# Memory attention of a decoder step: scores issued two units ahead of the turns, the low halves last, and the sample products moved to GpSimd

## The reference

```python
def memory_attention(h, mem_k, mem_v, w_mq, w_mo):
    q = jnp.einsum('btd,dhe->bthe', h, w_mq)
    s = jnp.einsum('bthe,bmhe->bhtm', q, mem_k).astype(jnp.float32) * (MEM_HDIM ** -0.5)
    p = jax.nn.softmax(s, axis=-1).astype(mem_v.dtype)
    o = jnp.einsum('bhtm,bmhe->bthe', p, mem_v)
    return jnp.einsum('bthe,hed->btd', o, w_mo)
```

## Time and profile before

| | |
|---|---|
| median of three runs | 1979.57 us |
| span of the profiled execution | 1973.4 us |
| what lies around the span (the difference) | 6.2 us |
| TensorE busy in the span | 95% |
| VectorE busy | 62% |
| ScalarE busy | 29% |
| GpSimd busy | 28% |
| mean granted TensorE clock | 0.985 of full speed |

### The profile page before, as it was taken

How to read it: one execution, slowest core, us unless ns; L and a number is a source line. 1 busy time by engine, 2 the same in 40 slices (tenths; PEclk the granted TensorE clock), 3 DMA queues, 4 the chain that set the end, 5 groups by cost and what they waited for, 6 DMA issues and landing times.

```text
span 1973.4 us, 35022 instructions
## 1 busy us (share of the span) xinstructions
PE 1875.2 (95%) x15121; PEld 1617.4 (82%) x15121; DVE 1215.5 (62%) x1579; ACT 567.5 (29%) x962; POOL 547.0 (28%) x384
## 2 busy tenths in 40 slices
PE   7999999998899899999998699998999999999999
PEld 7988888884566444448997589998999999999998
DVE  5585583675677888875433746884377177375475
ACT  5222221244444455552121332110011011021026
POOL 2212211240000243423224013433333333333540
PEclk8999999998999999999999899999999999999999
DMA  7211211133000798943124402111211211211202
GB/s 237 53 46 33 55 45 33 30 74 120 1 1 1 293 339 329 337 172 129 33 86 150 160 22 65 43 43 34 64 44 34 63 43 33 65 38 38 86 22 89
DMA packets 162310, 176.77 MB, mean 90 GB/s; under 512 B 21982, under 2 KB 146932, under 8 KB 157772
## 3 DMA queue, kind: packets, MB, share of 16 engines
q1 hardware_dynamic: 146240, 93.54, 16.1%
q0 software_dynamic: 7168, 75.50, 10.0%
q10 hardware_dynamic: 8750, 5.49, 0.9%
HBM read 161.33 MB, written 13.27 MB: 88 GB/s over the span
## 4 chain that ended last, share of the span: by engine, by line
PE 79%; DVE 13%; ACT 4%; issue 2%; DMA 1%; POOL 1%; ACTq 0%; DVEq 0%; POOLq 0%; SPq 0%
PE PS L769 18%; PE PS L771 18%; PE PS L770 18%; PE PS L1060 4%; PE PS L806 4%; PE PS L1093 3%; PE PS L1001 2%; PE PS L850 2%; DVE ct L2366 2%; PE PS L979 2%; PE PS L1050 1%; PE PS L1075 1%; DVE Sst L1939 1%; DVE small L2126 1%; DVE ct L2386 1%
## 5 line engine op out<-in xcount | busy, mean ns | idle before, releaser
L715 POOL CAST whi<-wraw 128x1024 fp32r<-128x1024 f32 (+4 forms) x142 | 139.9, 985 | 1019.4 <-PE PS L771 905.7
L769 PE MATMUL PS<-BH,whi 128*128 128x344 f32 x1152 | 368.9, 320 | 0.0
L770 PE MATMUL PS<-BL,whi 128*128 128x344 f32 x1152 | 367.1, 319 | 0.0
L771 PE MATMUL PS<-BH,wlo 128*128 128x344 f32 x1152 | 367.0, 319 | 0.0
L717 POOL TENSOR_TENSOR wlo<-wraw,whi 128x1024 fp32r<-128x1024 f32 (+4 forms) x142 | 309.1, 2177 | 11.4
L770 PEld LDWEIGHTS PS<-BL,whi 128*128 128x128 f32 x1152 | 216.2, 188 | 0.5 <-issue 0.5
L769 PEld LDWEIGHTS PS<-BH,whi 128*128 128x128 f32 x1152 | 216.2, 188 | 0.5 <-issue 0.5
L771 PEld LDWEIGHTS PS<-BH,wlo 128*128 128x128 f32 x1152 | 216.2, 188 | 0.0
L769 PE MATMUL PS<-XH,whi 128*128 128x344 f32 x528 | 180.3, 341 | 3.4 <-DVE XL L1826 3.4
L2274 DVE TENSOR_TENSOR XT<-PS,XT 128x1032 f32<-128x1032 f32 x48 | 59.2, 1232 | 179.7 <-PE PS L771 179.6
L770 PE MATMUL PS<-XL,whi 128*128 128x344 f32 x528 | 169.6, 321 | 0.0
(11 more groups left out here) (445 smaller groups left out, 3729.3 us busy)
## 6 DMA issues: line engine op xcount, KB each, us to landing
wraw<-in_w_up_dram SPq DMA_DIRECT2D x44, 512.0 KB, 3.9
wraw<-in_w_in_dram SPq DMA_DIRECT2D x20, 512.0 KB, 4.1
wraw<-in_w_down_dram SPq DMA_DIRECT2D x24, 256.0 KB, 2.8
wraw<-in_w_down_dram SPq DMA_DIRECT2D x16, 320.0 KB, 3.1
xt_kept<-XT SPq DMA_DIRECT2D x1, 4128.0 KB, 13.4
XT<-xt_kept SPq DMA_DIRECT2D x1, 4128.0 KB, 13.5
xstage<-in_x_prompt_dram SPq DMA_DIRECT2D x8, 512.0 KB, 10.1
wraw<-in_w_out_dram SPq DMA_DIRECT2D x8, 512.0 KB, 4.7
```

Source lines behind the costliest of these rows:

```text
L715: gp.tensor_copy(hi, raw).then_inc(w_hi_done, 1)
L769: pe.matmul(out, wh[:, t, 0:m], hi[:, tile(t), s], start=(t == first), stop=False)
L770: pe.matmul(out, wh[:, t, 0:m], low, start=False, stop=False)
L771: ins = pe.matmul(out, wl[:, t, 0:m], hi[:, tile(t), s], start=False, stop=(t == last))
```

## The change

Four things move together.

TensorE's unit becomes scores(n + 2), turn(n), values(n - 1): the scores no longer stand behind the turn and its wait. `keep_busy` is gone, 75 transposes in all. The banks of the scores get a counter of their own (`freed["ms"]`), as the order of scores and turns now differs between TensorE and ScalarE.

VectorE's unit becomes max(n + 2), scale(n + 1), the sample work, low(n - 1).

The product of keys and query goes to GpSimd, in place in the key buffer; VectorE keeps the sum. There are three key buffers, and the sample rows are taken in units 4 to 11 without a gap.

The softmax of the sample scores on VectorE and the turn on TensorE stand one unit later (12, 13, 14, 15 where 11, 12, 13, 14 stood on VectorE). On TensorE only the turn of the sample scores moves, from unit 11 to 12.

```diff
-            use(("ms", n), [n % 2], "s")
+            use(("ms", n), [n % 2], "ms")
...
-            use(("mpt", n), [2 + n % 2], "s")
             if n + 2 < len(munits):
                 plan_ms(n + 2)
+            use(("mpt", n), [2 + n % 2], "s")
...
-        sample_at = {2: 0, 3: 1, 4: 2, 6: 3, 7: 4, 8: 5, 9: 6, 10: 7}
+        sample_at = {4 + b: b for b in range(NS)}
...
-                        if b >= 2:
-                            sp.wait_ge(prod_done, b - 1)
-                            sp.dma_start(sK[b % 2][:, :, :], i["cache_mem_k"][0, b].rearrange("(t p) h e -> p t (h e)", p=P)).then_inc(sk_in[b % 2], 16)
+                        if b >= 3:
+                            sp.wait_ge(prod_done, b - 2)
+                            sp.dma_start(sK[b % 3][:, :, :], i["cache_mem_k"][0, b].rearrange("(t p) h e -> p t (h e)", p=P)).then_inc(sk_in[b % 3], 16)
...
+            def sample_products(b):
+                gp.wait_ge(sk_in[b % 3], 16 * (b // 3 + 1))
+                gp.tensor_tensor(sK[b % 3][:, :, :], sK[b % 3][:, :, :], QB[b][:, :].unsqueeze(1).broadcast_to([P, 2, ME]), ALU.mult).then_inc(prod_new, 1)
...
+                if j == job_no[("mo", 0)]:
+                    gp.wait_ge(q_in, 16 * NS)
+                    for b in range(NS):
+                        sample_products(b)
                 split_weight(j)
...
-                if n < 14:
-                    keep_busy(7, 6 if n < 11 else 3)
+                if n + 2 < len(munits):
+                    memory_scores(n + 2)
                 pe.wait_ge(m_new, n + 1)
                 turn(("mpt", n), [Pm[n % 2][:, hh, m * P:m * P + P] for hh in range(2) for m in range(2)])
-                if n + 2 < len(munits):
-                    memory_scores(n + 2)
                 if n:
                     memory_values(n - 1)
-                if n == 11:
+                if n == 12:
                     pe.wait_ge(prod_done, NS)
...
+                if n + 2 < len(munits):
+                    memory_max(n + 2)
                 if n + 1 < len(munits):
                     memory_scale(n + 1)
-                if n + 2 < len(munits):
-                    memory_max(n + 2)
-                if n:
-                    memory_low(n - 1)
                 if n in sample_at:
                     b = sample_at[n]
-                    ve.wait_ge(q_in, 16 * NS)
-                    ve.wait_ge(sk_in[b % 2], 16 * (b // 2 + 1))
-                    step(ve.tensor_tensor(prod[:, :, :], sK[b % 2][:, :, :], bc(QB[b][:, :], 1, 2), ALU.mult))
-                    ve.tensor_reduce(sc[:, :, MH * b:MH * b + MH], prod[:, :, :].rearrange("p t (h e) -> p t h e", h=MH), AX, ALU.add).then_inc(prod_done, 1)
-                    ve.wait_ge(prod_done, b + 1)
+                    ve.wait_ge(prod_new, b + 1)
+                    ve.tensor_reduce(sc[:, :, MH * b:MH * b + MH], sK[b % 3][:, :, :].rearrange("p t (h e) -> p t h e", h=MH), AX, ALU.add).then_inc(prod_done, 1)
...
+                if n:
+                    memory_low(n - 1)
```

More of the change, by code:

```diff
@@ L193, in build_program @@
         Pm = [Pm0, Pm1]
-        mko, PTm0, PTm1, QS, prod, sc, scr, pm, sK0, sK1, *sV = place(
+        mko, PTm0, PTm1, QS, prod, sc, scr, pm, sK0, sK1, sK2, *sV = place(
             B0, B1, ("mko", [P, 2, ME], F32), ("PTm0", [P, 4, P], F32), ("PTm1", [P, 4, P], F32), ("QS", [NS, ME], F32),
@@ L197, in build_program @@
             ("pm", [P, 2, 32], F32), ("sK0", [P, 2, ME], F32), ("sK1", [P, 2, ME], F32),
-            *[(f"sV{n}", [P, 2, ME], F32) for n in range(NS)])
-        PTm, sK = [PTm0, PTm1], [sK0, sK1]
+            ("sK2", [P, 2, ME], F32), *[(f"sV{n}", [P, 2, ME], F32) for n in range(NS)])
+        PTm, sK = [PTm0, PTm1], [sK0, sK1, sK2]
         QB = place(S0, A0, *[(f"QB{n}", [P, ME], F32) for n in range(NS)])
@@ L217, in build_program @@
         psum_full = {"d": sem("dense_full"), "r": sem("rec_full")}
-        freed = {n: sem(f"freed_{n}") for n in ("v", "s", "rv", "rs")}
+        freed = {n: sem(f"freed_{n}") for n in ("v", "s", "ms", "rv", "rs")}
         ident_in, consts_in = sem("ident_in"), sem("consts_in")
@@ L245, in build_program @@
         m_max, m_new, om_hi = sem("m_max"), sem("m_new"), sem("om_hi")
-        sk_in, sv_in = [sem(f"sk_in{n}") for n in range(2)], sem("sv_in")
+        sk_in, sv_in, prod_new = [sem(f"sk_in{n}") for n in range(3)], sem("sv_in"), sem("prod_new")
         q_out, q_in, qs_set, prod_done, s_max, s_exp, s_new2 = sem("q_out"), sem("q_in"), sem("qs_set"), sem("prod_done"), sem("s_max"), sem("s_exp"), sem("s_new2")
@@ L256, in build_program @@
         p_max, p_new = sem("p_max"), sem("p_new")
-        uses, nth, last_of = {}, {"d": 0, "r": 0, "v": 0, "s": 0, "rv": 0, "rs": 0}, {}
+        uses, nth, last_of = {}, {"d": 0, "r": 0, "v": 0, "s": 0, "ms": 0, "rv": 0, "rs": 0}, {}
         def use(key, banks, by):
@@ L653, in _ @@
                     full(sp, ("mq", MH - 1))
-                    for b in range(2):
+                    for b in range(3):
                         sp.dma_start(sK[b][:, :, :], i["cache_mem_k"][0, b].rearrange("(t p) h e -> p t (h e)", p=P)).then_inc(sk_in[b], 16)
@@ L1191, in memory_scores @@
                 end(ins)
-            def keep_busy(b, count):
-                for r in range(count):
-                    pe.transpose(PS[:, b, P * (r % 3):P * (r % 3) + P], ident[:, :], ident[:, :])
             def memory_values(n):
@@ L1666, in memory_exp @@
                                          bias=small[:, c:c + 1], accum_out=small[:, 8 + c:9 + c])
-                ins.then_inc(freed["s"], 1)
+                ins.then_inc(freed["ms"], 1)
             memory_exp(0)
@@ L2328, in _ @@
             for n in range(len(munits)):
+                if n + 2 < len(munits):
+                    memory_max(n + 2)
                 if n + 1 < len(munits):
                     memory_scale(n + 1)
-                if n + 2 < len(munits):
-                    memory_max(n + 2)
-                if n:
-                    memory_low(n - 1)
                 if n in sample_at:
                     b = sample_at[n]
-                    ve.wait_ge(q_in, 16 * NS)
-                    ve.wait_ge(sk_in[b % 2], 16 * (b // 2 + 1))
-                    step(ve.tensor_tensor(prod[:, :, :], sK[b % 2][:, :, :], bc(QB[b][:, :], 1, 2), ALU.mult))
-                    ve.tensor_reduce(sc[:, :, MH * b:MH * b + MH], prod[:, :, :].rearrange("p t (h e) -> p t h e", h=MH), AX, ALU.add).then_inc(prod_done, 1)
-                    ve.wait_ge(prod_done, b + 1)
-                elif n == 11:
+                    ve.wait_ge(prod_new, b + 1)
+                    ve.tensor_reduce(sc[:, :, MH * b:MH * b + MH], sK[b % 3][:, :, :].rearrange("p t (h e) -> p t h e", h=MH), AX, ALU.add).then_inc(prod_done, 1)
+                elif n == 12:
                     full(ve, "sct")
                     ve.tensor_reduce(small[0:32, 40:41], bank("sct")[0:32, 0:MT], AX, ALU.max, negate=True).then_inc(s_max, 1)
-                elif n == 12:
+                elif n == 13:
                     emptied(ve, "sct")
@@ L2348, in _ @@
                     ve.tensor_scalar(scr[0:32, :], scr[0:32, :], small[0:32, 42:43], None, ALU.mult).then_inc(s_new2, 1)
-                elif n == 13:
+                elif n == 14:
                     full(ve, "spt")
                     take(ve.tensor_copy(pm[:, :, :].rearrange("p m n -> p (m n)"), bank("spt")[:, 0:64]))
-                elif n == 14:
+                elif n == 15:
                     full(ve, "spv")
                     take(ve.tensor_copy(prod[:, :, :], PS[:, uses["spv"][1][0]:uses["spv"][1][0] + 2, :]))
+                if n:
+                    memory_low(n - 1)
             memory_low(len(munits) - 1)
```

## The result

| | median us | runs | ratio to before | 95% interval |
|---|---|---|---|---|
| before, beside it | 1978.78 | 4 | | |
| changed | 1952.86 (1950.26 to 1958.99) | 4 | 0.9877 | 0.9856 to 0.9898 |
| changed, measured again | 1954.34 (1948.52 to 1957.91) | 5 | 0.9868 | 0.9849 to 0.9888 |

The last row was measured beside a median of 1980.75 for the kernel before. The change made the kernel some 24 to 26 us faster, 1.2 to 1.3%. The forecast was a gain of 16.3.

A forecast was written before the change was run, and what follows sets the result against it. It took the loop as bound by a chain of waits across engines, no engine being full. 4.9 + 21.1 - 9.2 - 0.5 = 16.3 us gain, 1979.6 - 16.3 = 1963.3 us; 8-in-10 range 1953 to 1972.

The forecast's parts named there:

- the likeliest case: Whole kernel: gain of 12 to 20 us, time 1959.5 to 1967.5, chance 0.62.
- in step: GpSimd's products fall while VectorE does other work, no scale held: gain 26.0 - 0.5, time 1954.1, chance 0.17.
- the loop of about 51 us: Sign of being right: the loop over the 16 units, 67.44 us before, would take about 51 us.
- the long scales of 1.5 to 3 in about every second unit: Sign of being right: VectorE's scales in units 3 to 11, otherwise 0.69 us, lengthened about every second time.
- Plain unit 3.19 to 2.37: VectorE's new order hides scale and reciprocal in its wait for ScalarE: 0.82 us in each of 6 units, 4.9 us.
- Sample unit 5.69 to 3.05: Sample product off VectorE, round over ScalarE hidden: 2.64 us saved in each of 8 units, 21.1 us.
- Holds, 8 x 2.3 / 2 = 9.2: VectorE's scale waits for a GpSimd product in every second sample unit, 2.3 us each: costs 9.2 us.
- Clock, 0.5: TensorE in the loop, without the fill of transposes, sometimes drops to half clock: costs 0.5 us.
- The rival of a clock that stays down: Without the fill TensorE stays at 1.2 GHz from early in the loop: 7.6 us slower, 1987.2, chance 0.05.
- Reloads hidden with 2.6 to spare: Key reload some 4.2 us plus product 2.4 makes 6.6, its row wanted three units later at 9.2: no cost.
- Tail 8.46, weights' splits in time: Loop's end to first dense output product stays 8.46 us; GpSimd's output-weight splits hidden by 11 us and more.
- Around the span, 6.2: Profiled execution lies 6.2 us under the median of the runs, and the same distance was expected after the change.

The follow-up runs named there:

- tiny products: Changed kernel with each GpSimd product cut to one element in 1024 per partition: stage 48.41 us, median 1952.55 us.
- late first product: Changed kernel with one 128x1024 memset on GpSimd between the queries' arrival and the first product: stage 51.06 us, median 1955.66 us.
- two buffers: Changed kernel with two key buffers in place of three: stage 58.81 us, median 1960.11 us.
- doubled product: Changed kernel with each GpSimd product made twice, first into a scratch tile: stage 67.06 us, median 1970.76 us.
- the run with the scale on ScalarE: Changed kernel with the scales of units 5 to 12 made by ScalarE, reciprocals left on VectorE: stage 47.66 us, median 1950.34 us.
- the last run on the other chip: Changed kernel with scales of units 5 to 12 on ScalarE and the last five value loads behind the last key reload: 1978.49 us, ratio 0.9853.

## Why the prediction was off in size

The direction, the place and all the mechanisms of gain were right; the likeliest case was not. The forecast of 1963.3 priced 16.3 us, the runs show 24 to 26, and the rival "in step" with 1954.1 is what happened. The medians of the changed kernel, 1952.86 and 1954.34, lie at the low end of the range given, 1953. Of the signs named, the loop of about 51 us (41.93) and the long scales of 1.5 to 3 in about every second unit (one of 16) failed.

- *Plain unit 3.19 to 2.37:* 2.38 measured. Right.
- *Sample unit 5.69 to 3.05:* 2.85 measured. The instructions that follow one another on VectorE overlap by 0.08 at four places and not at two; the remaining 0.03 is a hundredth of a microsecond in each of three terms. Eight times 0.2: 1.6 us more than forecast.
- *Holds, 8 x 2.3 / 2 = 9.2:* this is the step that failed. The rows for it were read rightly (one engine waits for the other's instruction, and of VectorE's instructions in a sample unit only the scale is held), and so was the remark that 2.4 and the rest of VectorE's unit are near a tie. I took a coin toss for a near tie. The two are coupled: a product that starts under a scale is itself held, by 0.45, and then ends where the next scale begins. That state keeps itself, and only a product set free by something else (the queries, a late reload) leaves it. The prediction says that the trace agrees "in both directions", but the rows that it shows have only VectorE held; that GpSimd can be the one to wait is what the sum left out. The changed kernel's holds were 3.1 us: 1.95 against products and 1.19 against the splits. Of these 0.73 had its like before: 2.4 net. The tiny products put 1.5 to 1.9 on the products, and the late first product showed that a shift costs one hold of 0.98, not many.
- *Clock, 0.5:* the loop's granted clock rose from 0.90 to 0.96 and to 1.00 in the second profile. Without the fill TensorE is busy for 2.4 of 2.86 us. In the first profile there was one fall, after the wait of the held scale. Here is TensorE's timeline around it:

```profile
1110.00 1.03 PE L1198 MATMUL PS<-MKT,qm 128*128 128x256 f32 x4
1112.99 1.10 PE L814 MATMUL PS<-ident,Pm 128*128 128x128 f32 x4 [1.96 <-DVE Pm L2321]
1113.88 1.92 PE L1208 MATMUL PS<-PTm,MV 128*128 128x128 f32 x8
```

  The values took 1.92 as in the earlier trace rows, and the next unit still took 2.85. The rival of a clock that stays down didn't come; in an undisturbed unit TensorE waits only 0.44 us. But one long wait doesn't settle whether the clock falls: with the late first product TensorE waited 2.06 us at the same place and the clock stayed at 1.00. Where long waits came one after another, the loop's clock was lower: 0.90 with two buffers, 0.88 with the doubled product.
- *Reloads hidden with 2.6 to spare:* right when they land in 3.9, wrong for the later ones at 5.7 to 6.0, which the earlier trace rows didn't show at half the rate of loads. One of these, of 5.97, led to the one large hold.
- *Tail 8.46, weights' splits in time:* right for the dense product that needs them. That they hold two scales on their way, by 0.46 and 0.73, was not in the sum.
- *Around the span, 6.2:* wrong, it is 1.8 in every run after it. This did not move the forecast, which takes the gain off the median.

Together: 16.3 + 1.6 from the sample unit + 6.8 from the holds + 0.5 from the clock = 25.2, against the 25.5 of the first profile. The second profile, at 27.1, had shorter holds.

## What to carry to other kernels

When two engines can only use a resource in turn and their cycles are about equal, as here, don't price the wait as a matter of chance. Ask which of the two is held when they meet, and what starts each: an engine that asks just behind the other settles into the gap and pays with time it has; one that is started by something else (a transfer, a third engine) falls anywhere and can hold the one on the path. Ask also what the held instruction's successor waits for: a hold that only hides another wait costs nothing more. When transfers are put in another order, follow the ones that were pushed back. And compare the stage that was changed, from one landmark to another: two spans can differ by what a gather elsewhere took in that execution.

## What the runs showed of the hardware

- In none of these traces did a GpSimd product and a VectorE scale, which has two SBUF inputs, run side by side: whichever started first finished, 2.35 and 0.69 alone, up to 2.90 and 2.83 with a wait. A GpSimd cast with one input did the same: 0.61 alone, 1.07 to 1.16 when it started under a scale.
- A VectorE sum with one SBUF input ran across products at its 1.21. One input is not enough to be safe, though: the softmax scale of 32x256, with one SBUF tensor and a scalar for each partition, took 1.17 across a split in place of 0.34.
- A reload of 512 KB that lands in 3.6 to 4.0 us with one every 5.7 us takes up to 6.2 when there is one every 2.7 to 2.9 us. With no value load issued in between, most took 3.6 to 4.6, but single ones still 5.2 and 5.4.
- The same gather took much longer on another chip, in one profile on each. The maximum behind each of its 32 steps, in the run with the scale on ScalarE and then in the last run on the other chip: 220.5 against 248.6 us.

```profile
L2206 DVE TENSOR_REDUCE dsm<-PS x32: 652/692/693, 662.3 to 882.8; 128x1 f32<-128x512 f32 x32
```

```profile
L2209 DVE TENSOR_REDUCE dsm<-PS x32: 680/692/693, 664.4 to 913.0; 128x1 f32<-128x512 f32 x32
```
